# The last step of 24 modulation sums: moved from TensorE to VectorE, with one joint step at the end

## The reference

```python
c_act = jax.nn.silu(c)                       # 2048 numbers
for l in range(2):
    shift, scale, gate = jnp.split(c_act @ w_ada[l] + b_ada[l], 3, axis=-1)   # w_ada[l]: 2048 x 6144
    h = rms_norm_2(x, norm_w[l]) * (1.0 + scale[:, None, :]) + shift[:, None, :]
    ...
    x = x + gate[:, None, :] * y
```

## Time and profile before

| | |
|---|---|
| median of three runs | 2507.94 us |
| the profiled execution | 2507.58 us, of which the span of its instructions is 2505.8 us |
| TensorE busy | 2480.9 us, 99% of the span |
| TensorE's weight loads (beside its matmuls) | 2093.0 us, 84% |
| VectorE busy | 1889.1 us, 75% |
| ScalarE busy | 1236.4 us, 49% |
| halves 0 to 319 | from the start to about 1013 us |
| granted clock of TensorE | 1.00 in all slices |

### The profile page before, as it was taken

The page is one execution under the profiler, slowest core; times in us unless marked ns, Lnnn a source line. Parts: engine busy times, 40 slices in busy tenths (PEclk is TensorE's granted clock), DMA queues, the critical chain, the costliest instruction groups (busy, mean ns, idle before and its releaser), DMA issues.

```text
span 2505.8 us, 33399 instructions
## 1 busy us (share of the span) xinstructions
PE 2480.9 (99%) x12591; PEld 2093.0 (84%) x12591; DVE 1889.1 (75%) x3357; ACT 1236.4 (49%) x1825; POOL 17.3 (1%) x37
## 2 busy tenths in 40 slices
PE   8999999999999999999999999999999999999999
PEld 6888888888888888878888869888888898888887
DVE  7888988898888888675555557666986767678865
ACT  4444444444444444445555456553455665444553
POOL 0000000000000000000000000000000000000000
PEclk9999999999999999999999999999999999999999
DMA  8787778777877787655545436444446544444554
GB/s 310 258 296 276 258 264 299 279 260 262 295 268 262 266 295 251 213 183 168 160 156 175 166 105 199 159 135 141 162 156 188 176 155 153 146 139 151 167 169 135
DMA packets 266113, 517.03 MB, mean 206 GB/s; under 512 B 16624, under 2 KB 21072, under 8 KB 265312
## 3 DMA queue, kind: packets, MB, share of 16 engines
q1 hardware_dynamic: 264256, 508.43, 59.5%
q0 software_dynamic: 1696, 6.47, 1.0%
HBM read 512.76 MB, written 2.10 MB: 205 GB/s over the span
## 4 chain that ended last, share of the span: by engine, by line
PE 90%; DVE 7%; issue 2%; ACT 1%; DMA 0%; DVEq 0%; SPq 0%; ACTq 0%
PE proj L585 15%; PE proj L587 15%; PE proj L586 15%; PE proj L1239 8%; PE proj L1241 8%; PE proj L1240 8%; PE scores L715 3%; DVE w_lo L1862 2%; PE proj L1231 1%; PE proj L1233 1%; PE proj L1234 1%; PE proj L625 1%; DVE arena L1987 1%; PE proj L627 1%; PE proj L626 1%
## 5 line engine op out<-in xcount | busy, mean ns | idle before, releaser
L1862 DVE TENSOR_TENSOR w_lo<-w_raw,w_hi 128x1024 fp32r<-128x1024 f32 (+1 forms) x740 | 895.2, 1218 | 288.7 <-ACT w_hi L1280 230.6
L1280 ACT ACTIVATE w_hi<-w_raw 128x1024 fp32r<-128x1024 f32 (+1 forms) x740 | 774.7, 1053 | 622.4 <-PE proj L587 382.4
L585 PE MATMUL proj<-w_hi,xt_lo 128*128 128x512 f32 x1632 | 651.1, 399 | 4.6 <-DVE xt_lo L1877 4.5
L587 PE MATMUL proj<-w_hi,xt_hi 128*128 128x512 f32 x1632 | 637.6, 391 | 0.0
L586 PE MATMUL proj<-w_lo,xt_hi 128*128 128x512 f32 x1632 | 636.3, 390 | 0.0
L1239 PE MATMUL proj<-w_hi,xt_lo 128*128 128x512 f32 x976 | 395.6, 405 | 0.3 <-DVE w_lo L1862 0.3
L1241 PE MATMUL proj<-w_hi,xt_hi 128*128 128x512 f32 x976 | 381.1, 390 | 0.0
L1240 PE MATMUL proj<-w_lo,xt_hi 128*128 128x512 f32 x976 | 380.5, 390 | 0.0
L585 PEld LDWEIGHTS proj<-w_hi,xt_lo 128*128 128x128 f32 x1632 | 307.3, 188 | 66.2 <-DVE xt_lo L1877 6.3
L587 PEld LDWEIGHTS proj<-w_hi,xt_hi 128*128 128x128 f32 x1632 | 306.7, 188 | 65.7
L586 PEld LDWEIGHTS proj<-w_lo,xt_hi 128*128 128x128 f32 x1632 | 307.3, 188 | 60.5
(11 more groups left out here) (405 smaller groups left out, 2753.0 us busy)
## 6 DMA issues: line engine op xcount, KB each, us to landing
w_raw<-in_dsa_w_in_dram SPq DMA_DIRECT2D x159, 1024.0 KB, 7.5
w_raw<-in_w_in_dram SPq DMA_DIRECT2D x120, 1024.0 KB, 5.1
arena<-in_w_ada_dram SPq DMA_DIRECT2D x192, 512.0 KB, 6.1
w_raw<-in_w_out_dram SPq DMA_DIRECT2D x32, 1024.0 KB, 5.1
w_raw<-in_mla_w_in_dram SPq DMA_DIRECT2D x24, 1024.0 KB, 5.1
w_raw<-in_dsa_w_out_dram SPq DMA_DIRECT2D x16, 1024.0 KB, 5.0
w_raw<-in_mla_w_out_dram SPq DMA_DIRECT2D x16, 1024.0 KB, 5.1
w_raw<-in_mla_w_ukv_dram SPq DMA_DIRECT2D x8, 1024.0 KB, 5.4
```

The source lines that it names most:

```text
L585: mm(o, xt[1][:, k0 + kk, tok], WH[:, c % 2, k, 0:n], start=first, stop=False)
L587: ins = mm(o, xt[0][:, k0 + kk, tok], WH[:, c % 2, k, 0:n], start=False, stop=last)
L1280: A(hi[:, 2 * q:2 * q + 2, 0:n], RAW[:, c % 4, 2 * q:2 * q + 2, 0:n], ACT.Copy).then_inc(hi_made, 1)
L1862: V.tensor_tensor(lo[:, ks, 0:n], RAW[:, c % 4, ks, 0:n], hi[:, ks, 0:n].bitcast(F32), ALU.subtract).then_inc(lo_made, 1)
```

## The change

After it, VectorE adds up within groups of 32 partitions, and TensorE joins the four groups of partitions once for all 24 sums.

- A new VectorE function `fold(e, part)` takes 256 of the 512 columns of group e's accumulator. It turns each 32 x 32 block (`V.transpose`, 128 x 256) into the new tile `BLOCKS`, waits for that, and adds over runs of 32 (`V.tensor_reduce`, 128 x 256 to 128 x 8) into the new tile `FOLDS`. Two folds, 16 numbers in each partition, replace one `columns`.
- In `ada`, fold 0 of the group before stands in front of piece 0 of a group, and fold 1 in front of piece 1. The two folds of the last group stand in slot 320.
- `columns` and its calls are gone from TensorE. In slot 323 TensorE does four matmuls (96 stationary columns, 32 moving ones), in slot 325 VectorE copies 96 x 128 numbers to SBUF, and in slot 327 TensorE turns them with one matmul into `SP` columns 384 to 479. From there on all is as before.
- VectorE no longer waits for `ada_columned` before it uses an accumulator again; GpSimd waits for `ada_summed` (now: folded) in its place.

The folds stand in slots 19, 20, 34, 35, 45, 47, 60, 61, 71, 73, 85, 86, 97, 98, 109, 113, 123, 124, 138, 139, 148, 149, 163, 164, 173, 174, 185, 187, 201, 202, 213, 217, 226, 227, 241, 242, 251, 252, 261, 263, 277, 278, 289, 291, 302, 305, and twice 320.

```diff
+        FOLDS = take(DEPTH * ADA_COLS * 16, DSA_END)
+        BLOCKS = take(256)
+        SELECT = take(32)
...
-            def columns(e, seen):
-                l, b = e // ADA_COLS, e % ADA_COLS
-                pe.wait_ge(ada_summed, e + 1)
-                pe.wait_ge(max_found, seen + 1)
-                for q in range(4):
-                    at = 384 + 48 * l + 4 * b + q
-                    ins = mm(SP[:, at:at + 1], ACC[:, e % 2, q * P:(q + 1) * P], ONES[:, 0:1], start=True, stop=True,
-                             skip_group_check=True)
-                ins.then_inc(ada_columned, 1)
+            def join_folds():
+                yield DSA_HALVES + 3
+                pe.wait_ge(ada_summed, DEPTH * ADA_COLS)
+                pe.wait_ge(max_found, 48 + 1)
+                folds = FOLDS.rearrange("p (n r) -> p n r", r=4)
+                for r in range(4):
+                    ins = mm(SP[0:96, 32 * r:32 * r + 32], folds[:, :, r], SELECT, start=True, stop=True, skip_group_check=True)
+                ins.then_inc(ada_joined, 1)
+                yield DSA_HALVES + 7
+                pe.wait_ge(S("ada_join_copied"), 1)
+                mm(SP[:, 384:480], BLOCKS[0:96, 0:128], IDENT[0:96, 0:96], start=True, stop=True,
+                   skip_group_check=True).then_inc(ada_columned, 1)
...
+            def fold(e, part):
+                cols = slice(256 * part, 256 * part + 256)
+                own.sync()
+                own(V.transpose(BLOCKS, ACC[:, e % 2, cols]))
+                own.sync()
+                at = 16 * e + 8 * part
+                own(V.tensor_reduce(FOLDS[:, at:at + 8], BLOCKS.rearrange("p (n j) -> p n j", j=32), AX_X, ALU.add))
+                if part == 1:
+                    own.sync()
+                    dve.sem_inc(ada_summed, 1)
             def ada(slot):
                 for a in ada_pieces(slot):
                     e, k0 = a // ADA_K, 2 * (a % ADA_K)
-                    if k0 == 0 and e > 1:
-                        dve.wait_ge(ada_columned, e - 1)
+                    if e > 0 and k0 < 4:
+                        fold(e - 1, k0 // 2)
                     dve.wait_ge(ada_loaded[a % 3], 16 * (a // 3) + 16)
...
+                if slot == 6:
+                    own(V.tensor_reduce(SELECT, IDENT.rearrange("p (a j) -> p j a", a=4), AX_X, ALU.add))
+                if slot == DSA_HALVES:
+                    fold(DEPTH * ADA_COLS - 1, 0)
+                    fold(DEPTH * ADA_COLS - 1, 1)
+                if slot == DSA_HALVES + 5:
+                    dve.wait_ge(ada_joined, 1)
+                    V.tensor_copy(BLOCKS[0:96, 0:128], SP[0:96, 0:128]).then_inc(S("ada_join_copied"), 1)
```

More of the change, by code:

```diff
@@ L316, in program @@
         ada_used, ada_summed, ada_columned = sem("ada_used"), sem("ada_summed"), sem("ada_columned")
+        ada_joined = sem("ada_joined")
         rows_loaded, rows_turned, c_ready = sem("rows_loaded"), sem("rows_turned"), sem("c_ready")
@@ L361, in program @@
         PROWS = PTS[:, 0, 0:128]
+        FOLDS = take(DEPTH * ADA_COLS * 16, DSA_END)
+        BLOCKS = take(256)
+        SELECT = take(32)
+        assert spot[0] <= ARENA - 2 * D
         CQ = take(T * 1024, HEADS_END).rearrange("p (t n) -> p t n", t=T)
@@ L766, in windows @@
             def windows():
[L768 to L774, removed]
                 for i in range(DSA_ITERS):
@@ L792, in windows @@
                             ins.then_inc(done, 1)
-                            summed(B + at, 4 * a)
                         for k in range(6):
@@ L806, in windows @@
                                 attend(a * 4 + h, h % 2, lambda t: VN[:, t, h * P:(h + 1) * P])
-                            if k >= 4:
-                                summed(B + TICKS + 2 * k, 4 * a + 4)
-                summed(8 * DSA_HALVES, 48)
             def y_turns():
@@ L824, in y_turns @@
                         ins.then_inc(turned, 1)
-            side, turns = Side(windows()), Side(y_turns())
+            side, turns, folds_joined = Side(windows()), Side(y_turns()), Side(join_folds())
             for h in range(DSA_HALVES):
@@ L856, in _ @@
                     turns.upto(DSA_HALVES + 2 * n + q)
+                    folds_joined.upto(DSA_HALVES + 2 * n + q)
             last_block(C_DSA_OUT + 12, B_DSA_OUT + 3, turn_x, 2)
@@ L1989, in ada @@
                     dve.sem_inc(ada_used, 1)
-                    if k0 == 14:
-                        dve.sem_inc(ada_summed, 1)
             def windows():
@@ L2150, in _ @@
                     ada(slot)
+                if slot == 6:
[6 more added lines that the diff above has]
+                    V.tensor_copy(BLOCKS[0:96, 0:128], SP[0:96, 0:128]).then_inc(S("ada_join_copied"), 1)
                 if slot == DSA_HALVES + 16:
-                    dve.wait_ge(ada_columned, DEPTH * ADA_COLS)
+                    dve.wait_ge(ada_columned, 1)
                     dve.wait_ge(S("ada_rows"), 1)
@@ L2949, in spread @@
                 pool.dma_start(dst, src.partition_broadcast(P)).then_inc(done, 16)
-            pool.wait_ge(ada_columned, DEPTH * ADA_COLS)
+            pool.wait_ge(ada_summed, DEPTH * ADA_COLS)
             spread(LNG, io["ln_g"][0], par_loaded)
```

## The result

The changed kernel takes 2517.58 us (median of six runs, 2516.82 to 2518.82) against 2508.26 us of the kernel before on the same chips. The ratio is 1.0037, 95% interval 1.0027 to 1.0047: slower by 9.3 us, where 2508.6 and at most 2517 were forecast. So "no change that can be told" was wrong, and the time lies 0.6 us outside the range. The recorded execution has a span of 2515.6 us, 9.8 us longer.

The account below looks back on a forecast made before the run. The prediction took TensorE to be the bound, VectorE a close second: -21.0 + 20.2 + 0.4 + 1.0 = +0.6 us on 2507.58, and with the runs' median 0.4 above, 2508.6 us. The range was 2503 to 2517 us.

Parts of the forecast that it names:

- What goes from TensorE, -21.0: First stage: 24 `columns` leave TensorE, 22 at 0.82 us, two at 0.92, plus 1.1 us of waits: -21.0 us.
- The smallest margins: Lo part's end to the half's first matmul, smallest just before the windows: 1.46 us at half 102, 1.04 at 265.
- my table: Eight worst halves, each short by folds x 0.95 us plus `columns` gone less margin; the column adds up to 22.4 us.
- The price of a fold, 1.9 us a pair: On VectorE, first fold of a group 0.85 us, second 1.05, mean 0.95; 24 pairs are 46 us.
- The half-speed rival: VectorE's float32 turn runs at half speed, making VectorE the bound in most of the stage: 2517 us, chance 0.22.
- The stops, +20.2: TensorE standing still for late lo parts in the first stage: 22.4 us, less what VectorE's waits take back, +20.2 us.
- Fresh starts, +0.4: After a stop TensorE's first weight load is not hidden, 0.1 us, counted at the ends of some stretches: +0.4 us.
- Theory B: Rival account for the follow-up runs: each of some 60 TensorE stops costs about 0.13 us of fresh start, 8 us.
- The join, +1.0: TensorE after the first stage: four small matmuls at 0.82 us plus one more, +1.0 us; bounds 0.2 and 4.
- The unknown price: VectorE's turn, without a row: 2506 us at 0.347 us, 2517 at 0.692; 0.1 us per fold moves the sum 2.9.
- The rival that held the idle time to take the folds in full: VectorE's 82 us of waits absorb the folds, leaving -21.0 + 1.0: 2488 us, chance 0.07.
- The clock, rival 0.01: TensorE's clock falls for one half after each of eight groups of stops, 22 us: 2530 us, chance 0.01.

Follow-up runs that it names:

- e1: The changed kernel without the 48 turns and reductions, columns still gone and the join kept: 2490.34 us, ratio 0.9929 against the kernel before.
- e3: The changed kernel with ScalarE's window work (exponentials, copies) one half later in the first stage: 2512.25 us, ratio 1.0017 against the kernel before.
- e5: The changed kernel with one 128x512 fold per group in place of two: 2510.52 us, ratio 1.0010 against the kernel before.
- e2: The kernel before, all 24 columns kept, with 46 folds added on VectorE whose results nobody reads: 2526.64 us, ratio 1.0071.
- e4: The changed kernel with each piece's last VectorE operation signalling its own end (192 times): 2491.71 us, ratio 0.9935 against the kernel before.

## Why the prediction was wrong

The sums of the first stage can be read half by half, as the shift of each half's first matmul against the kernel before. At the 24 halves that had a `columns` in front the shift falls, by the gain; at all others it rises, by the stops.

| | at the 24 halves, us | at the others, us | half 320, us |
|---|---|---|---|
| forecast | -21.0 | +20.6 | -0.4 |
| changed kernel | -22.3 | +30.4 | +8.1 |
| e1, no folds | -23.0 | +3.7 | -19.6 |
| e3, loop opened | -22.5 | +25.6 | +3.1 |

(In e1 a difference of 0.3 us at the very start is left out.)

**What goes from TensorE, -21.0: too small, and right in e1 by luck.** A `columns` that is gone gives back 0.89 us and not 0.82. I took the time from its start to the next start, but the matmul in front of it is also followed sooner. From the last product with the values to the projection, before and after:

```profile
109.98 0.39 PE L732 MATMUL attended<-arena 128*128 128x128 f32 x2
...
111.02 0.47 PE L585 MATMUL proj<-w_hi,xt_lo 128*128 128x512 f32 x1
```

```profile
109.99 0.39 PE L737 MATMUL attended<-arena 128*128 128x128 f32 x2
110.13 0.47 PE L590 MATMUL proj<-w_hi,xt_lo 128*128 128x512 f32 x1
```

1.04 us have become 0.14. In e1, the gain of 23.0 us less 3.7 us of stops comes near what I had as 21.0 less 1.4.

**The smallest margins: misread.** I wrote that the margin is smallest just before the windows, 1.46 us at half 102 and 1.04 at half 265, and that no matmul of the projection waits for a lo part. But half 99 had 0.57 us, and half 252 had 0.05, with its first weight load held up by 0.28 us:

```profile
796.97 1.23 DVE L1862 TENSOR_TENSOR w_lo<-w_raw,w_hi 128x1024 fp32r<-128x1024 f32 x1 [0.24 <-ACT w_hi L1280]
...
798.25 0.19 PEld L585 LDWEIGHTS proj<-w_hi,xt_lo 128*128 128x128 f32 x1 [0.28 <-DVE w_lo L1862]
798.25 0.50 PE L585 MATMUL proj<-w_hi,xt_lo 128*128 128x512 f32 x1
```

In the stretch around it e1 stops TensorE for 2.6 us without any fold, where my table has stops by folds alone.

**The price of a fold, 1.9 us a pair: right.** The turn took 438 ns where I took 420, the reduction 420 where its row had 422, and behind the signal VectorE idles 0.22 us. Over halves 88 to 90 of the trace after, the lo parts become later by 0.81 and 1.12 us, 1.93 a pair. This is 0.4 us of the miss by my own 2.9 us per 0.1 us of a fold, 0.7 by the 4.4 of e5. The half-speed rival is dead. The Trainium skill, "VectorE: DVE Perf Modes", section "The three transpose paths", led the prediction to an estimate of 0.45 us. The measured 0.438 is nearer to that than to my 0.42.

**The stops, +20.2: the step that failed.** They came to 30.4 us, fresh starts included. They stood where I said, but every one of the eight stretches lost more than its row, with what VectorE's waits inside it were to take back already subtracted. A stretch here reaches from the end of the one before to the start of the next, without the halves that had a `columns` in front.

| worst half | forecast, us | changed kernel, us | e3, us |
|---|---|---|---|
| 46 | 0.7 | 1.0 | 1.7 |
| 77 | 1.1 | 2.5 | 1.2 |
| 102 | 4.0 | 5.3 | 4.5 |
| 153 | 2.4 | 3.7 | 3.2 |
| 182 | 4.0 | 4.4 | 4.8 |
| 233 | 1.9 | 3.6 | 2.3 |
| 265 | 5.1 | 7.1 | 6.6 |
| 313 | 1.0 | 2.8 | 1.3 |

The first matmul of half 102 now starts on the end of its lo part, 330.85 + 1.22 = 332.07:

```profile
330.85 1.22 DVE L1859 TENSOR_TENSOR w_lo<-w_raw,w_hi 128x1024 fp32r<-128x1024 f32 x1
...
332.12 0.50 PE L590 MATMUL proj<-w_hi,xt_lo 128*128 128x512 f32 x1 [1.06 <-DVE w_lo L1859]
```

The failing sentence is "a stretch begins where VectorE is fully ahead", with the waits that "take back" lateness. I took every wait of VectorE in the earlier trace rows as time to catch up. Those for ScalarE behind the maxima are not: ScalarE stands in VectorE's own loop. So stretches began with VectorE still late. At half 88, TensorE was 0.4 us earlier than before, and the lo part 0.2 us later, with no new fold since slot 73. e3 opens the loop and gives back 5.3 us: that part is shown. It gives nothing back in the first stretch and in that of half 182. The other 5 us of the stops are only argued: the price of a fold (0.4 to 0.7 us), the stops that e1 has beyond my 1.4 (2.3), and fresh starts beyond my 0.4 (at most 1.1, below) come to about 4, but no run takes them apart.

**Fresh starts, +0.4: there, and small.** Inside the stretches a stopped half starts 0.05 us behind its lo part, and a fresh start is hidden in the next stop. Where the next half is not stopped, it shows: half 103 had its lo part 0.44 us before it started, and was 0.15 us later still than half 102. There are ten such halves in the trace after (47, 71, 88, 103, 148, 151, 183, 260, 263, 311), with 0.13 to 0.17 us each, so 1.5 us at most. Theory B's price per stop was right; that every stop pays it was not.

**The join, +1.0: too small, 1.6.** It was within its bounds. Neither of its waits stopped TensorE. The four matmuls cost 1038.65 - 1037.39 = 1.26 us, start to start, where `columns` had 0.82. Their loads take 272 ns (median) in place of 192; their stationary operand is read with a stride of four numbers, but no run shows that the stride is the reason. The last matmul cost 0.14, and the half behind each of the two places loses another 0.12 us.

```profile
1037.39 1.42 PE L764 MATMUL scores<-arena 128*96 128x32 f32 x8
1038.65 0.47 PE L590 MATMUL proj<-w_hi,xt_lo 128*128 128x512 f32 x1
```

**The unknown price and the range.** I spread the range by the price of the turn alone and treated the sum as exact for a given price. The account of which waits give way was the weaker part, and it had no bounds. Its two ends were: no wait for ScalarE gives way, or all do. The first end is about what was measured, 2517.6, with a turn only 0.02 us dearer than I took it. With a turn of 0.692 us on top, the upper end belonged well above 2517; how far, I have not worked out. The rival that held the idle time to take the folds in full was wrong by the same error.

**The clock, rival 0.01.** The mechanism exists: in e2 waits of 1.0 and 1.3 us were followed by a stretch at a mean of 0.66. In the changed kernel's first stage the clock stayed at 1.00, so it explains none of the 8.1 us there. Behind it, where TensorE idles for 3 us in the rows below and idled for 4 before the change, at a clock of 1.00 (the stretch from 1100 us), it did fall in the recorded execution:

```profile
1125.00:1130.00 5.00, 3.10 (x12) 2.23 (x11) 4.57 (x9) 0.20 (x1) 0.00 (x0) 0.87 0.67 210
1130.00:1135.00 5.00, 3.96 (x17) 2.58 (x15) 3.12 (x5) 1.08 (x2) 0.00 (x0) 0.79 0.53 168
```

It costs 0.5 us there: the shift against the kernel before goes from 9.66 to 10.14. So the stretch at 1.00 that I held against this rival was one execution's, and not a sign that the clock stays up.

## What to carry to other kernels

A wait is room for more work only if what it waits for does not itself depend on the waiting engine: follow each wait back one step further before it is counted as idle time, and see in the trace whether such waits shrink when the engine is late. When work is moved off the bounding engine to the second busiest, the gain itself uses up the margin that was to hide the cost, so both have to be summed stretch by stretch. And before work is made smaller, look at how the engine's operations are signalled: 192 signals sent by the operation itself, in place of a wait and a separate signal, were worth 26 us here, more than the whole change, and nothing as long as that engine was not needed.

## What the runs showed of the hardware

- A float32 turn of 32 x 32 blocks on VectorE: 438 ns for 128x256, 704 to 706 ns for 128x512. By the difference that is 1.04 ns a column and some 170 ns fixed; a reduction of the same inputs took 420 and 686 ns, also 1.04 ns a column.
- On VectorE, a wait for the engine's own counter followed by a separate signal leaves 0.24 us idle in front of the next operation. An operation that signals at its own end lets the next one start 0.09 us before it has ended (e4).
- TensorE's granted clock fell to a mean of 0.66 over 5 us behind a wait of 1.0 us (e2, 405 us) and 1.3 us (e2, 740 us), at 1.6 us each, but not behind the many stops of 0.1 to 1.1 us in the changed kernel's first stage. Behind the same idle time after 1100 us it fell in the recorded execution of the changed kernel and not in that of the kernel before. What tells these apart stays open.
- The first matmul behind a stop is followed 0.34 us later (332.12 to 332.46) in place of 0.23, and the half is some 0.15 us longer.
- A stationary operand of 128 x 96 float32 numbers read with a stride of four took 272 ns to load, one of 128 x 128 without a stride 192 ns.
